# Inverting 32-row instead of 16-row diagonal blocks on GpSimd in a chunked delta-rule layer

## The reference, cut to what matters

```
lower = where(strict, (k_beta @ k.T) * decay, 0)        # per chunk of tokens
sol   = triangular_solve(lower + I, [v * beta, k_beta * exp(g)])
u, w  = sol[..., :DV], sol[..., DV:]
for each chunk: v_new = u - w @ state
                o     = (q * exp(g)) @ state + (q @ k.T * decay) @ v_new
                state = state * exp(g_last) + (k * exp(g_last - g)).T @ v_new
```

## Time and profile before

| | |
|---|---|
| median of 3 runs | 2379.15 us (2376.61 to 2381.82) |
| the profiled execution's own time | 2378.46 us |
| its span in the trace | 2376.8 us |
| PE, PEld busy | 97%, 81% |
| DVE, ACT, POOL busy | 59%, 52%, 10% |
| the delta layer's heads | about 40 us to 950 us of the span, 110.6 us from one head to the next |

### The profile page before, as it was taken

How to read it: one execution, slowest core, us unless ns; L and a number is a source line. 1 busy time by engine, 2 the same in 40 slices (tenths; PEclk the granted TensorE clock), 3 DMA queues, 4 the chain that set the end, 5 groups by cost and what they waited for, 6 DMA issues and landing times. The chain is left out here.

```text
span 2376.8 us, 35061 instructions
## 1 busy us (share of the span) xinstructions
PE 2312.5 (97%) x11550; PEld 1926.7 (81%) x11550; DVE 1396.4 (59%) x2573; ACT 1234.5 (52%) x2517; POOL 245.4 (10%) x387
## 2 busy tenths in 40 slices
PE   7999999999999998899999999999999999999989
PEld 6788888887888876678788888888888888888877
DVE  5766657575757573777672836547283654728341
ACT  5556555555556564465545545454554545454430
POOL 1202121211212120740000000000000000000000
PEclk9999999999999999899999999999999999999999
DMA  4122131312121211878212112111211211121151
GB/s 136 39 58 74 29 80 28 83 33 70 38 65 40 65 44 36 280 261 282 90 31 54 45 36 62 36 44 36 61 45 36 62 36 44 37 60 45 52 210 49
DMA packets 274927, 173.15 MB, mean 73 GB/s; under 512 B 69692, under 2 KB 256212, under 8 KB 274804
## 3 DMA queue, kind: packets, MB, share of 16 engines
q1 hardware_dynamic: 274804, 171.60, 24.6%
HBM read 144.12 MB, written 27.45 MB: 72 GB/s over the span
## 5 line engine op out<-in xcount | busy, mean ns | idle before, releaser
L373 PE MATMUL b_front<-g_h_hi,wb_w_hi 128*128 128x512 f32 x1280 | 511.0, 399 | 3.0 <-PEq L1329 3.0
L373 PE MATMUL b_front<-g_h_hi,wb_w_lo 128*128 128x512 f32 x1280 | 511.2, 399 | 0.0
L373 PE MATMUL b_front<-g_h_lo,wb_w_hi 128*128 128x512 f32 x1280 | 510.4, 399 | 0.0
L373 PE MATMUL a_proj<-g_h_hi,wa_w_hi 128*128 128x512 f32 x784 | 323.0, 412 | 4.0 <-ACT a_acc L720 1.8
L373 PE MATMUL a_proj<-g_h_lo,wa_w_hi 128*128 128x512 f32 x784 | 322.5, 411 | 0.0
L373 PE MATMUL a_proj<-g_h_hi,wa_w_lo 128*128 128x512 f32 x784 | 316.5, 404 | 0.0
L373 PEld LDWEIGHTS b_front<-g_h_hi,wb_w_hi 128*128 128x128 f32 x1280 | 241.3, 189 | 51.7 <-issue 3.3
L373 PEld LDWEIGHTS b_front<-g_h_hi,wb_w_lo 128*128 128x128 f32 x1280 | 241.3, 189 | 50.2
L373 PEld LDWEIGHTS b_front<-g_h_lo,wb_w_hi 128*128 128x128 f32 x1280 | 241.3, 189 | 49.1
L1949 ACT ACTIVATE b_acc<-b_front,g_gains 128x512 f32<-128x512 f32 x96 | 66.0, 688 | 288.9 <-DVE b_qk L2241 208.2
L2124 DVE TENSOR_TENSOR wb_w_lo<-wb_raw,wb_w_hi 128x1024 fp32r<-128x1024 f32 x79 | 96.0, 1215 | 140.2 <-ACT wb_w_hi L1897 140.2
(11 more groups left out here) (295 smaller groups left out, 4462.7 us busy)
## 6 DMA issues: line engine op xcount, KB each, us to landing
wb_raw<-in_b_w_in_dram SPq DMA_DIRECT2D x80, 512.0 KB, 3.8
p_w_raw<-in_a_w_out_dram SPq DMA_DIRECT2D x64, 512.0 KB, 4.1
wa_raw<-in_a_w_in_dram SPq DMA_DIRECT2D x48, 512.0 KB, 4.2
a_out<-a_og SPq DMA_DIRECT2D x64, 128.0 KB, 1.8
p_a_raw<-a_out SPq DMA_DIRECT2D x64, 128.0 KB, 4.8
a_zx<-inverse_tiles SPq DMA_DIRECT2D x16, 384.0 KB, 4.5
u_tiles<-a_u SPq DMA_DIRECT2D x8, 512.0 KB, 3.2
p_x<-in_x_dram SPq DMA_DIRECT2D x4, 1024.0 KB, 8.1
```

The source lines that it names most:

```text
L373: last = pe.matmul(out, w[:, k, :], a[:, k, ks], start=(n == 0), stop=(n == 23))
```

## The change

Blocks of 32 are inverted, so that two levels are left on TensorE. Now 32 blocks (8 tiles by 4) would fill 32 partitions; the kernel fills 128 by giving each block four times, once for each quarter of 8 of its 32 columns (`PARTS_OF_BLOCK`, `PART`). The elimination has 31 columns and 62 dependent instructions, of (31 - j) rows by min(j + 1, 8) columns: 6312 elements for each partition where there were 30 instructions and 1360 elements. The blocks are loaded in 4 DMAs instead of 1, and stored in 8 instead of 2.

A batch of the levels takes 4 slots instead of 6 and begins in slot 3, 7, 11, 15 instead of 1, 7, 13, 19. The decays move from slots 12 and 15 to 6 and 9, the k·k products from 16 and 19 to 11 and 14, so that `u` is written by VectorE in slots 12 and 15 instead of 17 and 20, and `u` is stored by SP in slot 16 instead of 21.

```diff
-BLK = 16
+BLK = 32
-LEVELS = 3
+LEVELS = 2
+PARTS_OF_BLOCK = P // BLK
+PART = BLK // PARTS_OF_BLOCK
...
-LEVEL0 = 1
-DECAYS = (12, 15)
+LEVEL0 = 3
+LEVEL_STEP = 2 * LEVELS
+DECAYS = (6, 9)
-K_GRAMS = (16, 19)
+K_GRAMS = (11, 14)
-BLOCKS_OUT = 21
-INVERSE_BACK = 34
+BLOCKS_OUT = 16
+INVERSE_BACK = 33
...
+        bxt = bd[:, 0:PART, :]
...
-                        sp.dma_start(bd[:, :, :], as_blocks(u_dram)).then_inc(blocks_in, 16)
+                        for q in range(PARTS_OF_BLOCK):
+                            sp.dma_start(part_of(bd, q), as_blocks(u_dram)).then_inc(blocks_in, 16)
...
-                        sp.dma_start(as_blocks(inv_dram[0]), bd[:, :, :]).then_inc(inv_out, 16)
-                        sp.dma_start(as_blocks(inv_dram[1]), bx[:, :, :]).then_inc(inv_out, 16)
+                        for q in range(PARTS_OF_BLOCK):
+                            sp.dma_start(as_blocks(inv_dram[1])[:, :, columns(q)], part_of(bx, q)).then_inc(inv_out, 16)
+                            sp.dma_start(as_blocks(inv_dram[0])[:, columns(q)], part_of(bxt, q)).then_inc(inv_out, 16)
...
-                    rows, width = BLK - 1 - j, j + 1
+                    rows, width = BLK - 1 - j, min(j + 1, PART)
```

More of the change, by code:

```diff
@@ L399, in delta_heads @@
         hw = m_.sb("hw", [P, 2, CONV, 4])
-        bd = m_.sb("bd", [NB * T, BLK, BLK])
-        bx = m_.sb("bx", [NB * T, BLK, BLK])
-        bt = m_.sb("bt", [NB * T, (BLK // 2) ** 2])
+        bd = m_.sb("bd", [P, BLK, BLK])
+        bx = m_.sb("bx", [P, BLK, PART])
+        bt = m_.sb("bt", [P, (BLK - PART) * PART])
+        bxt = bd[:, 0:PART, :]
         dec = m_.sb("dec", [P, T, P])
@@ L430, in as_blocks, with part_of, columns @@
                     .rearrange("p (j i) -> p j i", i=P)[:, :, 0:BLK])
+        def part_of(tile, q):
+            return tile[q * NB * T:(q + 1) * NB * T]
+        def columns(q):
+            return slice(q * PART, (q + 1) * PART)
         step = m_.ps("step", [P, 2, DV])
@@ L554, in body @@
                         if not (isinstance(n, int) and n == 0):
-                            sp.wait_ge(inv_out, n * 32)
+                            sp.wait_ge(inv_out, n * (32 * PARTS_OF_BLOCK))
                         sp.wait_ge(blocks_out, n * 16 + 16)
-                        sp.dma_start(bd[:, :, :], as_blocks(u_dram)).then_inc(blocks_in, 16)
+                        for q in range(PARTS_OF_BLOCK):
+                            sp.dma_start(part_of(bd, q), as_blocks(u_dram)).then_inc(blocks_in, 16)
                     if m is not None and (s - CHAIN0 - 8) % 3 == 0 and 0 <= (s - CHAIN0 - 8) // 3 < T:
@@ L566, in body @@
                         sp.wait_ge(lv_s, n * (LEVELS * T // 2) + 1)
-                        sp.dma_start(as_blocks(inv_dram[0]), bd[:, :, :]).then_inc(inv_out, 16)
-                        sp.dma_start(as_blocks(inv_dram[1]), bx[:, :, :]).then_inc(inv_out, 16)
-                        sp.wait_ge(inv_out, n * 32 + 32)
+                        for q in range(PARTS_OF_BLOCK):
+                            sp.dma_start(as_blocks(inv_dram[1])[:, :, columns(q)], part_of(bx, q)).then_inc(inv_out, 16)
+                            sp.dma_start(as_blocks(inv_dram[0])[:, columns(q)], part_of(bxt, q)).then_inc(inv_out, 16)
+                        sp.wait_ge(inv_out, (n + 1) * (32 * PARTS_OF_BLOCK))
                         for part, tiles in enumerate((slice(0, 2), slice(2, T))):
@@ L606, in invert_blocks @@
                 if not (isinstance(n, int) and n == 0):
-                    pool.wait_ge(inv_out, n * 32)
+                    pool.wait_ge(inv_out, n * (32 * PARTS_OF_BLOCK))
                 pool.sem_inc(carrier, 1)
@@ L611, in invert_blocks @@
                 pool.sem_inc(carrier, 1)
-                pool.tensor_copy(bx[:, :, :].rearrange("t j i -> t (j i)")[:, 0:BLK * BLK:BLK + 1],
-                                 g.ones[0:NB * T, 0:BLK]).then_inc(bstep, 1)
-                pool.wait_ge(blocks_in, n * 16 + 16)
+                for q in range(PARTS_OF_BLOCK):
+                    diag = part_of(bx, q)[:, columns(q), :].rearrange("t i c -> t (i c)")[:, 0:PART * PART:PART + 1]
+                    ins = pool.tensor_copy(diag, part_of(g.ones, q)[:, 0:PART])
+                ins.then_inc(bstep, 1)
+                pool.wait_ge(blocks_in, (n + 1) * (16 * PARTS_OF_BLOCK))
                 for j in range(BLK - 1):
                     pool.wait_ge(bstep, n * (2 * BLK) + (2 + 2 * j))
-                    rows, width = BLK - 1 - j, j + 1
+                    rows, width = BLK - 1 - j, min(j + 1, PART)
                     prod = bt[:, 0:rows * width].rearrange("t (i c) -> t i c", c=width)
@@ L626, in invert_blocks @@
                 pool.sem_inc(carrier, 1)
-                pool.tensor_copy(bd[:, :, :], bx[:, :, :].rearrange("t i c -> t c i")).then_inc(blocks_inv, 1)
+                pool.tensor_copy(bxt, bx[:, :, :].rearrange("t i c -> t c i")).then_inc(blocks_inv, 1)
                 pool.wait_ge(blocks_inv, n * 2 + 2)
@@ L664, in body @@
                     if m is not None:
-                        b, k = divmod(s - LEVEL0 - 1, 6)
-                        if 0 <= b < T // 2 and k % 2 == 0:
+                        b, k = divmod(s - LEVEL0 - 1, LEVEL_STEP)
+                        if 0 <= b < T // 2 and k in range(0, 2 * LEVELS, 2):
                             use = LEVELS * b + k // 2
@@ L939, in body @@
                     if m is not None:
-                        b, k = divmod(s - LEVEL0, 6)
-                        if 0 <= b < T // 2:
+                        b, k = divmod(s - LEVEL0, LEVEL_STEP)
+                        if 0 <= b < T // 2 and k < 2 * LEVELS:
                             level, second = divmod(k, 2)
@@ L1007, in body @@
                     if m is not None:
-                        b, k = divmod(s - LEVEL0 - 2, 6)
-                        if 0 <= b < T // 2 and k % 2 == 0:
+                        b, k = divmod(s - LEVEL0 - 2, LEVEL_STEP)
+                        if 0 <= b < T // 2 and k in range(0, 2 * LEVELS, 2):
                             level = k // 2
```

## The result

The changed kernel takes 2425.8 us (median of 4 runs, 2422.3 to 2429.0), the one before 2379.9 beside it: a ratio of 1.0196, with a 95% interval of 1.0181 to 1.0211. It is 46 us slower where 8 us less were forecast, and outside the range.

What follows compares the result with a forecast made beforehand. PE, busy 97% of the span, was taken to bound the kernel; 40.5 - 7.8 - 15.8 - 6.5 - 2 = 8.4 us off 2378.46 gave 2370.1, said as 2371; likeliest range 2361 to 2378, whole range 2346 to 2398.

Steps and rivals of the forecast that it cites:

- the sum's last: Whole kernel: takes the summed gain of 8.4 us off the profiled execution's 2378.46 us, giving 2370.1.
- The removed levels: Layer 1 on PE: 5.35 us a head less, 37.4 in seven bodies and 3.1 in the last, 40.5 us.
- 110.6 to 106.6: Distance from head to head in layer 1's loop: 110.6 - 5.35 + 1.3 = 106.6 us.
- X: Length of the inversion on GpSimd: 37.3 us, with bounds of 27.5 and 44.
- That GpSimd and VectorE slow each other down: In the inversion: VectorE's instructions with two SBUF inputs hold up GpSimd, 8.8 us of X.
- Is it in time?: Looped bodies, store of the inverse: 46.6 us available, 46.2 needed, so 0.4 us in hand.
- Rival B: Inversion late in every head; beyond X = 37.7 each us costs PE one in eight places; 2398 at X = 41; chance 0.34.
- What follows the inversion: Eight stores, later loads back and late weights: PE waits 1.3 us in each looped body, 7.8 in all.
- the first head: First head of layer 1, no recurrence beside it: PE waits 15.8 us for the inverse and what follows it.
- the last head: Last head of layer 1: store 5.0 us late, PE waits 8.0 us, 6.5 more than before.
- The moved products: Layer 1's decays and k·k products change slots: cost nothing, or half a slot, 1 us a head, if the cover is gone.
- the recurrence: Layer 1: VectorE gets five of its steps nearer together between slots 5 and 16; 2 us charged in all.

Runs made afterwards that it cites:

- the runs with 4 and 8 memsets: Changed kernel plus four or eight one-element memsets on VectorE at the start of layer 1's out-projection: 2421.9 us with four, 2367.7 us with eight.
- memsets on before: Kernel before plus one-element memsets on VectorE in layer 1's out-projection: ratio 1.0204 with 212, 1.0206 with 84, 1.0001 with 148, 1.0001 with 64.
- The edit meant to win it back: Changed kernel with eight memsets, first transposes of k in slot 21 instead of 22: 2370.2 us, ratio to before 0.9970.
- the early weights: Changed kernel with eight memsets, load of the next head's second unit of weights issued ahead of the inverse's stores: 2360.4 us, ratio to before 0.9933.
- the run with the longer inversion: Changed kernel with eight memsets, plus nine memsets on GpSimd ahead of each head's elimination, each waited for: 2383.3 us, ratio to before 1.0032.
- the one at 27 ahead: Kernel before plus 64 memsets on VectorE, one ahead of each split in layer 1's out-projection: ratio 1.0001.

## Why the prediction was wrong

**The step that failed** is the sum's last: "2378.46 - 8.4 = 2370.1". It takes the gain of layer 1 off the whole profile and so lets all that lies outside layer 1 stay as it was. The change removes 44 instructions from VectorE's stream, and this moved the attention loop from 37 behind a boundary to 7 ahead of one. All that is not layer 1 stood at nothing in the sum, without a reason given; it measured 56 us. With the position mended the kernel takes 2367.7 us against the 2371 forecast; the ratio 0.9961 is 9.3 us, the forecast gain 8.4. Shown by the runs with 4 and 8 memsets and by the memsets on before. No rival of mine was of this kind: all were about waits in layer 1.

**The removed levels** held. From `u` to `u` in the loop 111.5 us lay before (190.24 to 747.71, five steps) and 107.4 with the eight memsets (185.97 to 723.17): 4.1 a head, against 5.35 - 1.3 = 4.05. The forecast 110.6 to 106.6 had the right difference, but by luck: of the 1.3 us a body that it took off, 0.4 came (the 2.4 us below, over six), and 0.8 came from the wait for `kd`, which it had at nothing. Both added back give 5.3 for the removed products, as forecast.

**X** was 35.4 to 35.7 in seven heads and 37.6 in the first, 37.3 forecast. That GpSimd and VectorE slow each other down held. The product of 192 columns took 1.38 us (424.12 above) beside VectorE's remainder of the weights and a gate (423.63 to 426.05); the next product, of 184 columns, took 0.50. Beside the last of three convolutions (VectorE's L1095, 419.40 to 421.90) and just behind them, a product and a subtraction of the same 156 columns took:

```profile
421.43 0.79 POOL L634 TENSOR_TENSOR a_bt<-a_bd,a_bx 128x156 f32<-128x156 f32 x1
422.30 0.56 POOL L637 TENSOR_TENSOR a_bx<-a_bx,a_bt 128x156 f32<-128x156 f32 x1
```

VectorE's convolutions rose from 0.76 to 0.81 us in the mean.

**Is it in time?** Yes, with 3.1 us in hand instead of 0.4; 1.9 of the difference is X. Rival B's threshold lies where X is 3 us longer than measured.

**What follows the inversion** was sized too long. Eight stores took 4.3 us (forecast 4.8), the loads back began 5.7 behind the first store (8.1), since the landing came soon after the last issue. In the loop PE waited 2.4 us in all behind the subtraction with eight memsets, and in after 4.8 and once 1.3 behind ScalarE's copy, instead of 7.8. In the first head, with eight memsets, PE's two waits are 4.2 and 2.5 us, 6.7 against 15.8; but part of the rest came as a lower clock. Windows of PE with eight memsets:

```profile
100.00:125.00 25.00, 25.00 (x120) 1.00 0.00 1
125.00:150.00 25.00, 18.29 (x67) 0.73 0.51 116
150.00:175.00 25.00, 25.00 (x140) 1.00 0.00 0
```

The low clock stands in one piece, and its level is 0.50 (1.2 GHz):

```profile
134.55:148.20 13.65, 9.88 (x28) 0.50 0.70 184
```

It fell in the wait that ended at 135.79, and products of 512 columns start there 0.43 us apart instead of 0.23. PE was busy for 9.88 us of it and did half of what it does at 2.4 GHz: a further 4.9 us, an estimate. The prediction had no term for it. In the last head the wait was 5.0, 3.5 more than before, against 6.5.

**The moved products**, taken at nothing, cost something: PE waits 7.0 us for `kd` in the bank that the transposes share (before 0.3) and 2.4 once for `a_v`. Its waits for VectorE and ScalarE in the recurrence rose by 3.7, where 2 were charged. I named the risk ("1 us a head, if the cover is gone") and did not look at who else uses the bank: the transposes of v, one slot on. The edit meant to win it back failed.

So the layer's 9.3 us came from terms that were each off by 2 to 9 us, in both directions: 40.5 - 2.4 (loop) - 11.6 (first head, clock included) - 3.5 (last head) - 9.1 (`kd` and `a_v`) - 3.7 (recurrence) is 10.2 by the trace with eight memsets. That it came so near to 8.4 is partly luck. The first product of layer 1's out-projection shows how far one execution may be off: 960.9 before (958.8 to 961.2 in six kernels), and 956.0, 948.2, 950.7, 950.9 and 948.2 in five executions of the changed layer 1.

**The best version** is the changed kernel with eight memsets and the early weights: 2360.4 us, 0.7% under the kernel before and 2.6% under the change as it was made.

## What to carry to other kernels

An edit changes every engine's instruction stream behind it. Before a slower result is put down to the edit, look for "issue" among the waits of a loop that the edit does not touch, and compare the instruction packets in a window over this loop; if both are new, shift the loop by a few empty instructions and measure again. By the count that fits here, a loop of 294 instructions on VectorE needs no fetch from 91 of 128 starts; of the other 37 the two nearest to the boundary that were run cost 2% and the one at 27 ahead nothing. So a series of variants that is timed without this check ranks their positions along with their ideas. In a kernel bound by TensorE, look for the lower clock behind its longer waits: those of 4.2 and 6.4 us had it, while the looped bodies with waits up to 1.0 us ran at a granted clock of 1.00 (175 to 850 us, eight memsets).

## What the hardware showed that was not expected

- A jump back into code that is not resident cost VectorE 6.1 to 8.4 us of issue with 7 instructions ahead of the boundary (6.8 to 8.4 in after), nothing with 27; TensorE waited 6.4 us a time for it, and the iteration took 9.3 us more.
- In layer 1's loop (468 to 496 instructions on VectorE) there are 11 to 12 of these packets an iteration, in before as in after, without a stall on VectorE. The queue serves more than VectorE: 56 more instructions an iteration on GpSimd (the run with the longer inversion) made 45 packets of 37, so the packets there cannot be put down to one engine. With the early weights VectorE had one stall in this loop, of 4.4 us ahead of the remainder of the weights. ScalarE had two in before, each at its loop's start; TensorE waited 1.1 and 0.4 us behind them (timeline of ScalarE, before):

```profile
352.19 0.38 ACT L669 ACTIVATE a_bc<-a_first 128x256 f32<-128x256 f32 x1 [4.65 <-issue]
```

- Copies of 32 partitions by 8 elements on GpSimd took 1.66 us for four, one of 128 by 256 took 0.70.
